# Two edits around a recurrence's output projection and the last chunk of an MLP

## The reference, cut to what matters

```python
y_x = (jax.nn.gelu(h_x @ w_gate) * (rec_x[0] + rec_x[1])) @ w_out      # 1280 -> 1024
x = x + g2 * rms_norm_2(y_x, norm_g[1])
h = modulate_2(rms_norm_2(x, norm_g[2]), sh3, sc3)
x = x + g3 * rms_norm_2(jnp.square(jax.nn.relu(h @ w1)) @ w2, norm_g[3])
```

## Time and profile before

| | us |
|---|---|
| median of three runs (2238.02 to 2246.97) | 2241.66 |
| the profiled execution | 2246.59 |
| its span | 2244.5 |
| PE busy in the span | 2151.8 |
| ACT busy, DVE busy | 988.5, 1681.9 |

### The profile page before, as it was taken

One profiled execution on the slowest core, in us unless ns is written; L12 is line 12 of the kernel. 1 busy time (PEld: TensorE's weight loads), 2 busy tenths in 40 slices (PEclk: granted clock), 3 DMA queues, 4 the chain that ended last, 5 costly groups with the idle time before them and its releaser, 6 DMA issues.

```text
span 2244.5 us, 36184 instructions
## 1 busy us (share of the span) xinstructions
PE 2151.8 (96%) x15439; PEld 1988.7 (89%) x15439; DVE 1681.9 (75%) x2339; ACT 988.5 (44%) x1325; POOL 29.0 (1%) x33
## 2 busy tenths in 40 slices
PE   7999999999999999999999899999999998699998
PEld 7999987999999998799998678888878886589998
DVE  5899867788798877788777765777775667966664
ACT  3534434534443343443345663422222347754442
POOL 0000000000000000000000000000000001110000
PEclk8999999999999999999999999999999999899999
DMA  8999744798789864457764001354574231133662
GB/s 302 312 330 309 244 144 143 244 319 295 259 285 311 298 208 147 147 191 247 239 224 146 6 20 64 111 164 151 168 235 159 75 113 61 36 113 129 215 198 75
DMA packets 338632, 417.48 MB, mean 186 GB/s; under 512 B 9274, under 2 KB 263208, under 8 KB 338472
## 3 DMA queue, kind: packets, MB, share of 16 engines
q1 hardware_dynamic: 335360, 411.84, 55.5%
q10 hardware_dynamic: 3112, 3.33, 0.5%
HBM read 414.09 MB, written 1.05 MB: 185 GB/s over the span
## 4 chain that ended last, share of the span: by engine, by line
PE 47%; DVE 6%; ACT 3%; issue 2%; POOL 0%; DVEq 0%; ACTq 0%
PE pb L619 46%; ACT wh L1408 1%; DVE wl L2017 1%; PE pb L1245 1%; DVE ACC L2025 1%; DVE SM L2610 1%; DVE L_y L2025 0%; DVE RS L2109 0%; DVE T L2025 0%; DVE Hl L2025 0%; ACT L_y L1409 0%; ACT A_P L1871 0%; DVE Y L2025 0%; DVE T L2017 0%; ACT L1409 0%
## 5 line engine op out<-in xcount | busy, mean ns | idle before, releaser
L619 PE MATMUL pb<-Hh,wh 128*128 128x256 f32 (+1 forms) x2624 | 793.9, 303 | 15.3 <-DVE Hl L2025 6.2
L619 PE MATMUL pb<-Hl,wh 128*128 128x256 f32 (+1 forms) x2624 | 777.9, 297 | 0.0
L619 PE MATMUL pb<-Hh,wl 128*128 128x256 f32 (+1 forms) x2624 | 776.1, 297 | 0.0
L2017 DVE TENSOR_TENSOR wl<-raw,wh 128x2048 fp32r<-128x2048 f32 (+3 forms) x271 | 601.0, 2221 | 184.9 <-ACT wh L1408 184.0
L1408 ACT ACTIVATE wh<-raw 128x2048 fp32r<-128x2048 f32 (+3 forms) x271 | 502.5, 1855 | 361.3 <-PE pb L619 264.5
L619 PEld LDWEIGHTS pb<-Hh,wh 128*128 128x128 f32 x2624 | 502.7, 192 | 34.3 <-issue 12.2
L619 PEld LDWEIGHTS pb<-Hl,wh 128*128 128x128 f32 x2624 | 503.0, 192 | 15.1 <-issue 2.2
L619 PEld LDWEIGHTS pb<-Hh,wl 128*128 128x128 f32 x2624 | 501.6, 192 | 12.8
L619 PE MATMUL pb<-Bh,wh 128*128 128x256 f32 (+1 forms) x1376 | 420.4, 306 | 8.1 <-DVE Y L2017 2.5
L619 PE MATMUL pb<-Bh,wl 128*128 128x256 f32 (+1 forms) x1376 | 414.0, 301 | 0.0
L619 PE MATMUL pb<-Bl,wh 128*128 128x256 f32 (+1 forms) x1376 | 413.9, 301 | 0.0
(11 more groups left out here) (249 smaller groups left out, 2107.1 us busy)
## 6 DMA issues: line engine op xcount, KB each, us to landing
raw<-in_ada_w_dram SPq DMA_DIRECT2D x126, 1024.0 KB, 5.6
raw<-in_ffn_w_in_dram SPq DMA_DIRECT2D x88, 1024.0 KB, 6.7
raw<-in_mlp_w_dram SPq DMA_DIRECT2D x64, 1024.0 KB, 5.4
raw<-in_ffn_w_out_dram SPq DMA_DIRECT2D x32, 1024.0 KB, 6.4
raw<-in_mix_w_in_dram SPq DMA_DIRECT2D x22, 1024.0 KB, 5.9
raw<-in_ffn_w_out_dram SPq DMA_DIRECT2D x16, 768.0 KB, 5.5
raw<-in_attn_w_qkv_dram SPq DMA_DIRECT2D x12, 1024.0 KB, 6.9
raw<-in_lru_w_in_dram SPq DMA_DIRECT2D x10, 1024.0 KB, 5.1
```

Source lines behind the costliest of these rows:

```text
L619: return e.matmul(o, l, r, start=st, stop=sp, skip_group_check=True)
L2017: return e.tensor_tensor(o, a, b, f)
```

## The change

There are two edits. **The projection:** `LO_STEPS` puts all four first halves ahead of all four second halves. The two output tiles of j = 0, 1 and 2 share one bank (0, 1, 2), those of j = 3 have banks 3 and 4, and bank 5 takes fillers. `Gh` comes in two parts, tiles 0 to 4 behind the roots of j = 3 and tiles 5 to 7 ahead of the last two sigmoids; `Gl` of 0 to 7 moves ahead of the last multiplication of `gated(4)`. ACT splits the third unit in the place of the old `Gh`, and two more behind the roots of j = 4; DVE subtracts one ahead of `one_less(4)` and one each behind the second and third scan group of j = 4. The first second half runs input tile by input tile, its tiles 5 to 7 ahead of the last scans. The fillers are 3, 4, 2 and 8 in four places. **The end:** XC is transposed ahead of the last chunk's m2 units and copied to T. In that chunk the squares are summed with the squares as weights and one column of ones (one sum per token and partition), Y times its gate (`G_y`) is transposed as it comes, and DVE forms each output tile as transposed G_y * 1/root + T. The last adaLN segment is due four units earlier. The diff, cut:

```diff
-LO_STEPS = [(0, 0), (1, 0), (2, 0), (0, 1), (1, 1), (2, 1), (3, 0), (3, 1)]
+LO_STEPS = [(j, hlf) for hlf in range(2) for j in range(4)]
...
+            if c == 3:
+                need((1, 1, 5))
...
-        "lo": (0, 1, 2, 3, 4, 5), "fin": (0, 1, 2, 3)}
+        "lo": (0,), "fin": (0, 1, 0, 1, 0, 1, 2, 3)}
+LO_BANKS = {0: (0,), 1: (1,), 2: (2,), 3: (3, 4)}
...
+            def turn_tiles(src, kts, ps, last):
+                for b in range(2):
+                    for kt in kts:
+                        ins = e.transpose(ps[b][:, 128 * (kt % 4):128 * (kt % 4) + 128], src(kt)[:, 128 * b:128 * b + 128], IDN)
+                    if last:
+                        full(ins, "fin")
+            def last_chunk(hid, need):
+                E.wait_ge("x", E.n["x"])
+                for g in range(2):
+                    ps = [fill("fin") for _ in range(2)]
+                    turn_tiles(lambda kt: XC[:, kt, :], range(4 * g, 4 * g + 4), ps, True)
+                sums = bank(SUMS_BANK, "rs.sqrt")
+                def tail(m):
+                    for kt in (2 * m, 2 * m + 1):
+                        E.wait_ge("sq", E.up("sq"))
+                        for b in range(2):
+                            ins = mm(sums[:, b:b + 1], T[:, 4 + kt % 4, 128 * b:128 * b + 128], KM[:, K_ONE:K_ONE + 1], kt == 0 and b == 0, kt == 7)
+                        ins.then_inc(sems["sq.read"], 1)
+                    E.wait_ge("gy", 2 * m + 2)
+                    if m % 2 == 0:
+                        ys[:] = [fill("fin") for _ in range(2)]
+                    turn_tiles(lambda kt: G_y[:, kt, :], (2 * m, 2 * m + 1), ys, m % 2)
+                ys = []
+                for m in range(4):
+                    fm("m2", "m2", hid, 256, need, said="y")
+                    if m:
+                        tail(m - 1)
+                tail(3)
...
-            stay(0, 36)
+            stay(0, 3)
...
+                order = [(kt, m) for kt in range(nk) for m in range(2)] if (j, hlf) == (0, 1) else [(kt, m) for m in range(2) for kt in range(nk)]
+                for kt, m in order:
...
+                    if (j, kk, m) == (0, 8, 0):
+                        stay(5, 8)
...
+                if (j, hlf) in ((2, 0), (3, 0)):
+                    stay(5, 4 if j == 2 else 2)
...
-            mods((1, 1, 1, 5))
-            sums.add()
...
+            mlp(1, 256, [4] * 4, h_need(), late=((1, 1, 1, 5),))
...   ScalarE
+                                if h == 0:
+                                    E.wait_ge("hid", nscr[0])
+                                    for x in range(4):
+                                        act(T[:, (0, 2, 1, 3)[x], :], full("fin")[:, :], ACT.Copy).then_inc(sems["fin.read"], 1)
+                                E.wait_ge("y", E.n["y"])
+                                for kt in (ft, ft + 1):
+                                    square(kt, Y[:, kt, 0:256], 256)
+                                for kt in (ft, ft + 1):
+                                    act(G_y[:, kt, :], Y[:, kt, 0:256], ACT.Copy, scale=S_GX[:, kt:kt + 1]).then_inc(sems["gy"], 1)
...
+                        if (j, g, w2) == (4, 3, 0):
+                            E.wait_ge("gg", 8)
+                            act(Gh[:, 5:8, :], L_g[:, 5:8, :], ACT.Copy).then_inc(sems["g.hi"], 1)
...
-                    E.wait_ge("gg", 8)
-                    act(Gh[:, 0:8, :], L_g[:, 0:8, :], ACT.Copy).then_inc(sems["g.hi"], 1)
+                    ahead("lo")
...
+                if j == 3:
+                    E.wait_ge("gg", 5)
+                    act(Gh[:, 0:5, :], L_g[:, 0:5, :], ACT.Copy).then_inc(sems["g.hi"], 1)
+            ahead("lo")
+            ahead("lo")
...
+            E.wait_ge("sq.read", nsq[0])
+            act(RS[:, 0:2], PB[SUMS_BANK][:, 0:2], ACT.Sqrt, bias=EPSC, scale=1.0 / D).then_inc(sems["rs.sqrt"], 1)
...   VectorE
+                    if (j, g) == (4, 3):
+                        E.wait_ge("g.hi", 2)
+                        tt(Gl[:, 0:8, :], L_g[:, 0:8, :], f32(Gh[:, 0:8, :]), ALU.subtract).then_inc(sems["g.lo"], 1)
...
+                    if j == 4 and g in (1, 2):
+                        ahead("lo")
...
+                ahead("lw")
                 if j == 3:
-                    E.wait_ge("g.hi", 1)
-                    tt(Gl[:, 0:8, :], L_g[:, 0:8, :], f32(Gh[:, 0:8, :]), ALU.subtract).then_inc(sems["g.lo"], 1)
-                ahead("lw")
+                    ahead("lo")
...
-            gate_of(S_GX, 1, 1, 5, 3)
-            add_normed(256, [(0, S_GX)])
+            E.wait_ge("rs.sqrt", E.up("rs.sqrt"))
+            E.step(e.reciprocal(RS[:, 0:2], RS[:, 0:2]))
+            E.wait_ge("fin.read", 4)
+            own()
+            for g in range(2):
+                for b in range(2):
+                    E.wait_ge("fin.full", 4 + 2 * g + b + 1)
+                    o = T[:, 2 * b + g, :]
+                    stt(o, PB[(0, 1, 2, 3)[2 * g + b]][:, :], RS[:, b:b + 1], o, ALU.mult, ALU.add).then_inc(sems["res"], 1)
```

More of the change, by code:

```diff
@@ L330, in build @@
                   "o2.read", "m1.read", "sqr.in", "y.act", "y", "lg.read", "lr.act", "lr.read", "lw.read", "lo.read",
[L331 removed]
+                  "u.hi", "u.lo", "iu", "th", "ex", "a2", "om", "root", "scan", "gg", "g.hi", "g.lo", "fin.read", "gy", "res"]
         sems = {n: ctx.enter_context(nc.semaphore("s_" + n.replace(".", "_"))) for n in names}
@@ L1139, in mlp @@
                     E.up("hid", chunks[c] * 2 // per)
-                    if c == last:
+                    if c == last and n == 512:
                         sums = Sums(n)
@@ L1164, in mlp @@
                         return seam
-                    else:
+                    elif c < last:
                         for m in range(4):
                             fm("m2", "m2", hid_at(b), n, hid_need, said=said)
-                            if c == last:
-                                sums.add(2 * m)
-                return sums
+                    else:
+                        mods(*late)
+                        last_chunk(hid_at(b), hid_need)
             between = cx_open()
@@ L1365, in _ @@
                 if hlf == 0:
-                    ib[j] = [RING["lo"][(2 * j + m) % 6] for m in range(2)]
-                    ib[j] = [bank(b, "lo.read") for b in ib[j]]
+                    ib[j] = [bank(b, "lo.read") for b in LO_BANKS[j]]
                 vh, vl, nk, ncol = weights("lo")
[L1369 to L1375, removed]
+                two = len(ib[j]) == 2
+                order = [(kt, m) for kt in range(nk) for m in range(2)] if (j, hlf) == (0, 1) else [(kt, m) for m in range(2) for kt in range(nk)]
+                for kt, m in order:
+                    c = slice(128 * m, 128 * m + 128)
+                    kk = 5 * hlf + kt
+                    o = ib[j][m][:, 0:256] if two else ib[j][0][:, 256 * m:256 * m + 256]
+                    if (j, kk, m) == (0, 8, 0):
+                        stay(5, 8)
+                    E.wait_ge("g.lo", 1 if kk < 8 else kk - 6)
+                    ins = mm3(o, (vh[:, kt, c], vl[:, kt, c]), (Gh[:, kk, :], Gl[:, kk, :]), kk == 0 and (two or m == 0), kk == 9)
+                    if kt == nk - 1:
+                        full(ins, "lo")
                 spent()
+                if (j, hlf) in ((2, 0), (3, 0)):
+                    stay(5, 4 if j == 2 else 2)
                 if hlf == 1:
@@ L1988, in _ @@
             half[0] = half[1] = [("gg", 10)]
-            for j, hlf in LO_STEPS:
+            for _ in range(3):
                 ahead("lo")
-                if hlf == 0:
-                    continue
+            for j in range(4):
                 for m in range(2):
@@ L1995, in _ @@
                     E.wait_ge("g.lo", 3)
-                    act(Y[:, 2 * j + m, 0:256], PB[RING["lo"][(2 * j + m) % 6]][:, 0:256], ACT.Copy).then_inc(sems["lo.read"], 1)
-                    E.wait_ge("lo.read", E.up("lo.read"))
-                    square(2 * j + m, Y[:, 2 * j + m, 0:256], 256)
+                    if j == 3:
+                        act(Y[:, 6 + m, 0:256], PB[LO_BANKS[3][m]][:, 0:256], ACT.Copy).then_inc(sems["lo.read"], 1)
+                    elif m:
+                        act(Y[:, 2 * j:2 * j + 2, 0:256], PB[LO_BANKS[j][0]][:, :].rearrange("p (h n) -> p h n", h=2), ACT.Copy).then_inc(sems["lo.read"], 1)
+                    if j == 3 or m:
+                        E.wait_ge("lo.read", E.up("lo.read"))
+                    if j == 3:
+                        square(6 + m, Y[:, 6 + m, 0:256], 256)
+                if j < 3:
+                    for m in range(2):
+                        square(2 * j + m, Y[:, 2 * j + m, 0:256], 256)
+                if j in (1, 2):
+                    ahead("lo")
             root_mean(256)
@@ L2514, in mlp @@
                     ft = 0
+                    if c == last and n == 256:
+                        gate_of(S_GX, 1, 1, 5, 3)
+                        own()
                     for h in range(2 if n == 512 else 4):
@@ L2766, in _ @@
```

(4 more changed lines are left out.)

20 lines of the change are left out of this document (5 added, 15 removed).

## The result

The changed kernel takes 2230.82 us (median of nine runs, 2226.22 to 2234.49) against 2241.06 for the kernel before (nine runs): a ratio of 0.9953, 95% interval 0.9939 to 0.9967, or 10.2 us less. The forecast was 12.1 less, 2229.6. The profiled execution took 2232.99 us, its span is 2230.6.

The account below looks back on a forecast made before the run. PE, busy 96% of the span, was taken to bound the kernel. The projection's -9.9 and the end's -2.2 sum to -12.1 us, from the median 2241.7 to 2229.6 us; range 2225 to 2238.

Parts of the forecast that it names:

- rival 1: Projection: the clock falls at the 2.95 us gap ahead of the fourth unit; total -10.7, 2231.0 us; chance 0.23.
- the forecast case: Whole kernel: both edits pay and the clock stays up at the gap; -12.1, 2229.6 us; chance 0.45.
- term 1: Projection: fewer products left behind the last scans; -9.9 us if the clock stays, -8.5 with a fall.
- term 2: End of the kernel: a shorter tail behind the last product, more work ahead of it; -2.2 us, from 0 to -3.
- I take no fall: Gap of 2.95 us ahead of the fourth unit: the clock stays up, with products and fillers on both sides.
- 2.45 didn't: Argument against a clock fall at the 2.95 us gap: a gap of 2.45 kept products 0.12 apart.
- Eight fillers, 1.6 us longer than the tiles 8 and 9 need: Projection, behind the products of tiles 5 to 7: fillers run to 1997.0, tiles 8 and 9 ready about 1995.4.
- weight splits don't replace PE there: Last three projection units: ACT 1.26 and DVE 1.48 us per unit against PE's 3.6, so PE stays the limit.
- Rival 2: End: transposes and waits ahead of the last chunk drop the clock; that edit +1.2, total -8.7, 2233.0 us; chance 0.14.
- Rival 3: Last scans: the two splits within them wait for ACT's high parts; price up to 3 us, 2232.6; chance 0.12.
- Rival 4: Slower: half clock through the projection's second halves and sums; all of it to the root gives 2254; chance 0.06.
- the moved adaLN loads cost nothing: MLP: same four loads and 16 DVE instructions, covered by PE; uncovered, 3.0 us for the one ahead of the last chunk.

Follow-up runs that it names:

- p6: Changed kernel with the fifth unit's low part made behind the last scans, nine fillers ahead of that unit and none ahead of tile 8: 2226.68 us, measured once.
- p8: Changed kernel with the second half of the transposes of x moved behind the last chunk's first product unit: 2231.93 us, measured once.
- p7: Changed kernel without its 17 fillers: 2235.53 us, measured once.
- p4: Changed kernel with nine fillers in place of four ahead of the fourth unit, to close the gap there: 2228.55 us, measured once.
- p1: Kernel before with the projection's edit alone, its end the old one: ratio 0.9966, median 2234.81 us against 2241.29.
- p9: Changed kernel with nine fillers ahead of the fourth unit, four instead of eight ahead of tile 8, x turned in two halves: 0.9948 of the kernel before, 2231.59 us.
- p3: Kernel before with its 36 fillers replaced by 128 transposes of the identity: 2242.86 us, measured once.
- p2: Kernel before with the end's edit alone: ratio 0.9986, median 2239.51 us against 2241.29.
- p10: p9 with the sixth unit's high part made on ACT between the Gh of tiles 8 and 9: 2226.06 us against 2238.44 for the kernel before, 0.9945.

## Why the prediction was right, point by point

**The sum.** -12.1 was forecast, -10.65 is in the traces and -10.2 in the medians. The sign and the size were right, and the time lies inside the range. What happened in the profiled execution is rival 1, with a chance of 0.23, and not the forecast case: the sign named for it, a PEclk of 0.50 behind the first gap, is there. That its -10.7 is what the traces show is in part luck, since term 1 with a fall was 0.5 too good (-8.5 against -8.0) and term 2 0.4 too poor. And that the median came within 1.2 us of the forecast is luck too: a second measurement of the same kernel gave 4.7 less than before, not 10.2.

**Term 1, the projection: -9.9 forecast, -8.0 measured.** The step that failed is "I take no fall" at the gap ahead of the fourth unit. The clock fell behind a gap of 2.2 us in all four executions that had it (the changed kernel twice, p6, p8) and behind 3.96 in p7, and p4, without the gap, gives 1.3 back, where 1.4 was priced. Without a fall the term is -9.3 (p4) or -9.7 (p1). The reason given for no fall was that "2.45 didn't". That was one execution: in ten of the twelve profiled ones the clock fell behind this very gap, and the kernel before happened to be one of the two without (last section).

The rest is small. The early scans were forecast 1.1 us earlier and are 0.9 earlier against the mark: I took 5.75 us from the first squares to the last `one_less` because DVE would be idle beside them, but it is 6.0, the first square itself taking 1.65 with DVE idle for the last microsecond of it. The last Gl was forecast 1.6 us later than before, against the mark, and is 1.9 later. PE's start was forecast at once behind the fillers, but it waits 0.8 for Gl, which made the gap 2.23 instead of 2.95. Gl was forecast 1.2 us ahead of the last sigmoid, and DVE starts it 0.4 ahead, when it is done with the multiplications before it. In p1, where the clock came back 8.6 us ahead of the mark and not 9.5, the mark lies 0.9 later against DVE's work: Gl starts 1.26 ahead of it, and the last `one_less` comes 10.27 behind it, against 10.66 in p4. These 0.4 us are the whole difference between -9.7 and -9.3.

"Eight fillers, 1.6 us longer than the tiles 8 and 9 need" named about the right excess (1.8 in p4, without a fall), but with another price. Halving them (p9 against p4) gave 0.9, since the next wait, the sixth unit's low part, stood 0.7 behind. I had written that weight splits don't replace PE there, by comparing rates (1.26 and 1.48 against 3.6); the rates were right, and the start of the first split was not looked at. That was a wait hidden under the fillers, and it becomes visible only when they go.

**Term 2, the end: -2.2 forecast, -2.6 measured** alone and in the whole. From the root to the last product it was forecast 5.65 longer and is 5.4. The pieces: 4.7 ahead of the last chunk was 4.5, with the wait for the copies at 0.9 against 1.0 (p8 takes it away and gains 1.08); the last product to the end was 8.6 and is 8.4. Root and reciprocal of two columns, which no row had shown, take 0.26 and 0.17, 0.5 with the way between them, as estimated.

**The rivals.** Rival 2 with the transposes falls: 16 of them take 0.13 each at full clock ahead of the chunk, and 128 keep the clock in p3. Rival 3 falls: DVE didn't wait inside the scans. Rival 4 falls: the lower stretch lasted 3 us. That the moved adaLN loads cost nothing was not tested alone, since both p2 and the changed kernel move them; but root to last product grew by 5.4, less than the 5.65 forecast with nothing for them, which leaves no room for the 3.0 us that they would cost uncovered.

## What to carry to other kernels

When first halves of products are pulled ahead of a serial chain, the gain is the PE work removed from behind it, and it must be counted from the moment at which PE can go on without a break: look for each input of the next units (here the high part made on ACT in program order) and not only at rates. Fillers ahead of a wait should fit the wait; those in one place were too few here (a gap of 2.2 us cost 1.3 in clock) and in another too many (1.8, or 3 with the fall, of which halving them gave back 0.9), and removing the excess shows the next wait. A sum of squares per token, taken as one column, with the scaling put off to the last instruction and x transposed early, shortens a serial tail even where it adds work to PE ahead of it: 5.4 us more in front, 8.0 less behind. Which of these three parts pays was not tested one by one.

## What was not expected of the hardware

A gap of 2.23 us between products let the clock fall to 0.50 for some 3 us in four executions out of four, while one of 2.79 in p1, one of 2.08 in p7 and one of 2.45 in the kernel before didn't. So the length of a gap alone doesn't decide. The last of these is the best witness, since it stands 187 to 190 us ahead of the mark in all twelve profiled executions, with the same code around it. The clock fell behind it in ten of them and stayed at 1.00 in two, the kernel before and p1. The changed kernel, against the earlier trace rows:

```profile
1779.47 0.36 PE L623 MATMUL pb<-Hh,wh 128*128 128x256 f32 x1 [2.46 <-DVE Hl L2085]
...
1780.00:1782.00 2.00, 2.00 (x11) 1.89 (x10) 1.20 (x4) 2.00 (x5) 0.00 (x0) 0.50 0.00 0
```

The same gap in the same code keeps the clock or loses it, from one execution to the next. The four falls behind 2.2 us aren't four independent trials: in all four the clock had last come back 9.5 to 9.6 us ahead of the last sigmoid, in p1 8.6. It fits a fall that depends on where a gap lies against earlier changes of the clock, but nothing here varied that place by itself, and it stays open. One execution without a fall is no evidence that a gap is safe.

Single-precision transposes (128x128) cost 0.11 each in a row in p3 and kept the clock at its upper level for 14 us.

Kernels that are alike up to there reached the last sigmoid of j = 4 anywhere from 1960.97 to 1971.59 us in twelve profiled executions, while the two stretches behind it repeated within 0.2 and 0.02 us where the code was the same. Most of the spread of whole runs, 8 us in the changed kernel, can arise ahead of any change near the end. It goes along with the granted clock: the earliest mark (p6) had 61 us at the lower level ahead of it and the latest (p7) 92, and the fifteen runs of the kernel before beside p10 go from 2233.48 us at a mean granted clock of 0.985 to 2250.41 at 0.976. What sets that was not tested. For effects of 1 to 3 us at the end of such a program, stretches between fixed marks of a trace say more than medians of whole runs.
